# Moving the start addresses of on-chip tiles in a one-core transformer layer: three filler tiles

## What is computed

```python
m = silu(cond) @ w_mod + b_mod            # six rows of 2048 for each of two conditions
z = (x * (1 + sc1) + sh1) @ w_in          # 8 heads q, k, v; latent q 512, latent kv 512, rope key 64
o = concat(neighbourhood_attention(z), mla_attention(z)) @ w_o
x = layernorm(ALPHA * x + g1 * o)
gate, up = split((x * (1 + sc2) + sh2) @ w_gu)   # 2 x 5632 columns
y = layernorm(ALPHA * x + g2 * (silu(gate) * up) @ w_down)
```

## Time and profile before

| | |
|---|---|
| median of 3 runs | 2891.59 us (2889.24 to 2893.04) |
| span of the profiled execution | 2891.1 us |
| TensorE matmul busy | 2814.6 us, 97% |
| TensorE weight load busy | 2494.9 us, 86% |
| VectorE busy | 1889.6 us, 65% |
| ScalarE busy | 1043.8 us, 36% |
| GpSimd busy | 187.9 us, 6% |
| mean granted TensorE clock | 0.987 |

### The profile page before, as it was taken

One profiled execution on the slowest core, in us unless ns is written; L12 is line 12 of the kernel. 1 busy time (PEld: TensorE's weight loads), 2 busy tenths in 40 slices (PEclk: granted clock), 3 DMA queues, 4 the chain that ended last, 5 costly groups with the idle time before them and its releaser, 6 DMA issues.

```text
span 2891.1 us, 42097 instructions
## 1 busy us (share of the span) xinstructions
PE 2814.6 (97%) x15844; PEld 2494.9 (86%) x15844; DVE 1889.6 (65%) x2939; ACT 1043.8 (36%) x1814; POOL 187.9 (6%) x262
## 2 busy tenths in 40 slices
PE   7899999999999999799999999999999999999996
PEld 2679999877888776799999999999999888888885
DVE  8766666585885787866666666666666555424337
ACT  7422333224453213644444444444444312112121
POOL 1121111000001000000000000000000000000005
PEclk9999999999999999899999999999999999999998
DMA  9754333352334655122222222222222535223231
GB/s 383 274 186 154 125 128 132 122 191 71 104 110 173 220 175 182 63 101 97 101 101 101 99 98 101 101 99 92 96 101 101 198 119 174 80 89 137 80 124 73
DMA packets 105768, 379.82 MB, mean 131 GB/s; under 512 B 14062, under 2 KB 14466, under 8 KB 103754
## 3 DMA queue, kind: packets, MB, share of 16 engines
q1 hardware_dynamic: 89088, 317.36, 30.9%
q0 software_dynamic: 16000, 61.06, 6.0%
q10 hardware_dynamic: 586, 0.12, 0.0%
HBM read 346.97 MB, written 33.48 MB: 132 GB/s over the span
## 4 chain that ended last, share of the span: by engine, by line
PE 90%; DVE 4%; DMA 2%; ACT 2%; issue 1%; SPq 0%; ACTq 0%; DVEq 0%
PE ps L1955 16%; PE ps L1957 16%; PE ps L1956 16%; PE ps L2455 12%; PE ps L2453 12%; PE ps L2454 12%; DMA mraw<-in_wstream 2%; PE ps L2154 1%; PE ps L2119 1%; DVE ps L1883 1%; PE ps L2102 1%; DVE acc L1885 1%; DVE stat L1933 0%; PE ps L2150 0%; PE ps L2093 0%
## 5 line engine op out<-in xcount | busy, mean ns | idle before, releaser
L2453 PE MATMUL ps<-actl,ringh 128*128 128x320 f32 x1408 | 435.5, 309 | 3.9 <-DVE ringl L1754 3.9
L2454 PE MATMUL ps<-acth,ringh 128*128 128x320 f32 x1408 | 435.1, 309 | 0.0
L2455 PE MATMUL ps<-actl,ringl 128*128 128x320 f32 x1408 | 435.1, 309 | 0.0
L2453 PE MATMUL ps<-acth,ringh 128*128 128x320 f32 x1056 | 327.1, 310 | 7.6 <-DVE ringl L1754 7.6
L2454 PE MATMUL ps<-actl,ringh 128*128 128x320 f32 x1056 | 326.9, 310 | 0.0
L2455 PE MATMUL ps<-acth,ringl 128*128 128x320 f32 x1056 | 326.8, 309 | 0.0
L1955 PE MATMUL ps<-dwh,fring 128*128 128x512 f32 x820 | 319.4, 390 | 1.0 <-DVE dwl L1858 1.0
L1957 PE MATMUL ps<-dwh,fring 128*128 128x512 f32 x820 | 319.2, 389 | 0.0
L1956 PE MATMUL ps<-dwl,fring 128*128 128x512 f32 x820 | 319.1, 389 | 0.0
L1858 DVE TENSOR_TENSOR dwl<-raw,dwh 128x1024 fp32r<-128x1024 f32 x82 | 100.4, 1224 | 291.4 <-ACT dwh L1319 291.4
L1754 DVE TENSOR_TENSOR ringl<-raw,ringh 128x512 fp32r<-128x512 f32 x264 | 181.7, 689 | 162.8 <-ACT ringh L1253 162.8
(11 more groups left out here) (310 smaller groups left out, 5775.0 us busy)
## 6 DMA issues: line engine op xcount, KB each, us to landing
raw<-in_wstream SPq DMA_DIRECT2D x503, 512.0 KB, 3.3
mraw<-in_wstream SPq DMA_DIRECT2D x64, 512.0 KB, 7.7
fscr<-fst POOLq DMA_DIRECT2D x44, 320.0 KB, 2.4
fst<-fscr SPq DMA_DIRECT2D x21, 640.0 KB, 4.1
acc<-in_xT SPq DMA_DIRECT2D x8, 640.0 KB, 16.0
oscr<-ost POOLq DMA_DIRECT2D x16, 320.0 KB, 2.5
ostage<-oscr POOLq DMA_DIRECT2D x16, 320.0 KB, 3.9
acc<-in_xtok POOLq DMA_DIRECT2D x4, 1280.0 KB, 7.4
```

The costliest lines, as they stand in the source:

```text
L2453: mm(out, ringh[:, s, w], ah, start=first, stop=False, skip_group_check=True)
L2454: mm(out, ringh[:, s, w], al, start=False, stop=False, skip_group_check=True)
L2455: ins = mm(out, ringl[:, s, w], ah, start=False, stop=last, skip_group_check=True)
```

## The change

Three tiles that nothing reads or writes are added, so that later tiles start elsewhere. No instruction is added, removed or moved: on each of the five engines the built program lists the same operations on the same tiles in the same order.

```diff
@@ -211,6 +211,7 @@
         bcols2 = sb("bcols2", [P, 2 * KD], f32, wsc)
         conds = sb("conds", [P, 2, KD, 2], f32, wsc)
         unit = sb("unit", [P, 3], f32, wsc)
+        sb("to_128", [P, 24], f32, wsc)
         grow = sb("grow", [2, 512], f32, wsc)
         mod1 = sb("mod1", [P, 2 * KD, 2], f32, wsc)
 
@@ -289,9 +290,10 @@
 
         f2 = ExitStack()
         fring = sb("fring", [P, 7, 2, 2, T], f32r, f2)
+        sb("dw_to_2k", [P, 32], f32, f2)
         dwh = sb("dwh", [P, 2, 1024], f32r, f2)
         dwl = sb("dwl", [P, 2, 1024], f32r, f2)
-        pad0 = sb("pad0", [P, 20480 // 4 - 4096], f32, f2)
+        pad0 = sb("pad0", [P, 20480 // 4 - 4096 - 32], f32, f2)
         gate2 = sb("gate2", [P, 2, D], f32, f2)
         tmp2 = sb("tmp2", [P, 2, 512], f32, f2)
         rowsb = sb("rowsb", [P, D], f32, f2)
@@ -304,6 +306,7 @@
         xsc.close()
 
         ysc = ExitStack()
+        sb("ring_to_2k", [P, 32], f32, ysc)
         ringh = sb("ringh", [P, 4, 512], f32r, ysc)
         ringl = sb("ringl", [P, 4, 512], f32r, ysc)
         xb = sb("xb", [P, 8, P], f32, ysc)
```

## The result

The changed kernel takes 2897.74 us (median of 13 runs, 2894.4 to 2899.43), the kernel before 2892.92 us (median of 13 runs on the same chips, 2889.24 to 2893.57). The ratio is 1.0016 with a 95% interval of 1.0009 to 1.0024: some 5 us slower, within the 0.2% that the prediction counts as no change, and not the 14 us faster that it forecast. The profiled execution after took 2897.18 us with a span of 2895.6 us, so 1.6 us lie outside its span. That holds for the kernel before too: of its later runs, the one of 2892.57 us has a span of 2891.0. The text ahead of the prediction set its span of 2891.1 us beside the median without this difference, which puts the forecast about 1 us too low and changes nothing else.

A forecast was written before the change was run, and what follows sets the result against it. TensorE, busy 97% of the span, was taken as the bound, through how fast matmuls follow each other. 6.4 + 6.4 + 1.2 + 0.8 - 0.8 = 14.0 us off 2891.1 gave 2877.1, as median 2877.6 us; range 2872 to 2893.

The forecast's parts named there:

- The step that failed: 512-column fp32r matmuls: each pays some 7 ns when its stationary slice starts off a multiple of 128 bytes.
- the moving operand does not seem to matter: Moving operand's address has no effect: 320-column matmuls with it 32 bytes off run 146.7 ns, gate and up's pace.
- `hh`: Values and latent projections: 320 triples gain 20 ns each, 6.4 us, by taking the remainders of the fast down projection.
- `oh`: Output projection: 320 triples gain 6.4 us, as `oh` comes to remainder 256, a multiple of 128.
- `ckvh`, `qlh` and the scores: Stages reading `ckvh` and `qlh` gain 1.2 us, latent attention's score matmuls 0.8 us, from addresses at multiples of 128.
- The rings: Gate and up (`ringh`) and down projection (`dwh`): moving the rings to multiples of 2048 bytes changes nothing, 0 us.
- The moved `dwh` loses: Rival, down projection: the distance between both operands' remainders counts, so 16.4 us are lost, time 2894; chance 0.05.
- What is late next: Two chunk ends: TensorE's shorter blocks wait for VectorE's split, 0.4 us more each, giving back 0.8 us.
- a rule against any gain: The skill's 16-byte SBUF lines and address-independent matmul pace (216 ns at 512 columns): no stage gains, sum 0.

The follow-up runs named there:

- e8_widths: Not the layer: the streams of e4_table with 256 to 512 moving columns, and with plain fp32; one run, 745.5 us.
- e4_table: Not the layer: TensorE alone runs fp32r streams, 128 stationary and 512 moving columns, at 16 x 16 start remainders; one run, 1692.5 us.
- e5_off32: e3_oh384 with `whi`, `hh`, `oh`, `ckvh` and `qlh` together 32 bytes off a multiple of 128; 2880.32 us, ratio 0.9959 to the kernel before.
- e6_dw256: e3_oh384 with `dwh` and `dwl` 256 bytes further on, `fring` unmoved; 2879.19 us, ratio 0.9955 to the kernel before.
- e3_oh384: e1_to128 plus a filler of 128 bytes ahead of `oh`, so `oh` meets `whi` at difference 0; 2879.12 us, ratio 0.9956 to the kernel before.
- e2_rings: The kernel before with the two ring fillers alone, without `to_128`; 2907.12 us, ratio 1.0051.
- e7_scores: e3_oh384 with `mx` and `rs` placed earlier, moving `qh` and `kh` to remainder 384 by 512; 2880.98 us, ratio 0.9960 to the kernel before.
- e1_to128: The kernel before with the filler `to_128` alone, both rings where they were; 2883.52 us against 2892.57, ratio 0.9970.

## Why the prediction was wrong

**The step that failed** is the sentence in bold: that a matmul pays when its stationary slice starts off a multiple of 128 bytes, with "the moving operand does not seem to matter" behind it. It rested on one contrast, the down projection (384 against 384) with the others (288 or 160 against 384). In that contrast the stationary remainder and the difference between both operands change together, so it can't tell them apart. What seemed to exclude the moving operand was taken at 320 columns, where e8_widths shows the same pace at every difference: the comparison could not have come out otherwise. What counts, at 512 columns, is the difference by 256 bytes: some 227 ns at 0 against 232.4 at 128 and 233.3 at 96 and 224 (e4_table, e5_off32, e6_dw256).

**`hh`, right.** The term "copies a measured case", and so it held under either rule, which makes its success no evidence for the one in bold: 6.4 us forecast, 3.1 + 2.6 = 5.7 us measured. By the table it is 960 x (233.4 - 227.7) = 5.5 us.

**`oh`, mis-sized through the same step.** 6.4 us forecast, 2.3 us measured. The argument "before, `oh` at 160 and `hh` at 288 paid the same" had a second reading: both were at a bad difference, 224 and 96. The change took `oh` to 128, a third bad one. The table gives 960 x (233.3 - 232.4) = 0.9 us, and the steps of the stage itself at full clock fall by as much, from 233.3 to 232.4 ns on average. The rest, 1.4 us, is the shorter time at the lower clock (1.5 us, less 0.1 us of longer waits), which e2_rings has as well without any change to this stage's addresses: so even the 2.3 us are in good part luck. With difference 0 (e3_oh384) the stage is 6.9 us shorter than before, as the term had it.

**`ckvh`, `qlh` and the scores.** 1.2 us forecast, 1.1 us measured. Scores: 0.8 us forecast, 0.1 us measured. The filler moves both operands of each by the same 96 bytes, so their difference stayed what it was, 128 between `kl_` and `qh`. With that at 0 (e7_scores) the stage gives 0.4 us.

**The rings.** For `ringh` the 0 was right: 684 matmuls in 100 us, 1090.63 us for the stage. For `dwh` it was not, +13.8 us. The mechanism stood in the text as the rival *The moved `dwh` loses*, at 16.4 us, and got a chance of 0.05. The steps of the timelines, 232.2 after against 226.7 in the earlier trace rows, give 2460 x 5.5 = 13.5 us. That rival's time was 2894, with all the gains of the forecast left in. By its own rule `oh` and the scores gain nothing (6.4 and 0.8 us), and then nothing is given back at the chunk ends (0.8 us), which I had not worked through: 2894 + 6.4 + 0.8 - 0.8 gives 2900, beside 2898 measured. It was given too little: the 0 for `dwh` copied no case, since no large operand of the trace before stood at remainder 0, and the same text noted that.

**What is late next, right in kind, but not reached.** VectorE's split at two chunk ends was to cost TensorE 0.4 us each once its blocks were shorter. In the changed kernel they hardly were, and the two waits together came to 0.9 us, beside 0.41 + 0.39 = 0.8 us before. In e3_oh384, where the blocks are as short as forecast, they are 0.65 and 0.78 us, the second of which was 0.39 us in the earlier trace rows.

The Trainium skill was weighed in the prediction as a rule against any gain. By its page SBUF — State Buffer (Who interferes with whom), TensorE has two independent read ports, one for the moving operand and one for weight loads. From that alone one would expect no effect of where the two stand to each other. The trace shows one with all else idle, 226.7 against 233.4 ns (e4_table); whether it arises at the ports no run shows. The 16-byte lines of the same page (Specifications) give no reason for it either, since every address here is a multiple of 32. The 216 ns that the prediction took from TensorE: Matmul & The Clock Gate (Back-to-back issue gap) is that section's figure for an isolated matmul; the best stream here takes 226.7 ns.

**What stays open** is whether a matmul's own two operands are the pair that counts or its moving operand and the next one's stationary slice, since all three matmuls of a triple had the same remainders in every run that decides; which part of the memory or of TensorE's fetch has the period of 256 bytes, why difference 64 pays only 1.6 ns, and the 0.9 us that the changed kernel starts later (99.62 to 100.54 us at the first value matmul; the tiles in use up to there have the same addresses in e1_to128, which has 99.38 us).

## What to carry to other kernels

For a stream of fp32r matmuls with 128 stationary and 512 moving columns, list for each operand pair the difference between the two start addresses by 256 bytes and bring it to 0; 2.9% of the pace of such a stage hangs on it, and a round address of one operand alone brings nothing and can spoil a pair that was good. Stages of 320 moving columns, and plain fp32 at 512, showed no effect; with 64 or 32 stationary columns difference 0 brought nothing. A contrast between two stages shows that something differs, not what: before a rule is read from it, list everything that differs between them, test a suspect where the effect exists, and where it can be done measure the grid by itself: 256 pairs took one run of 1.7 ms here.

## What the runs showed of the hardware

All at a granted clock of 1.00 but for the 427 ns, which is a step at 0.50. Two streams of triples with 128 stationary and 512 moving columns that differ only in the addresses of their operands run at 226.7 or up to 234.2 ns a matmul. Even the best pair stays 13.3 ns above 512 / 2.4 = 213.3 ns. At 320 columns the excess is the same 13.3 ns whatever the addresses (146.7 against 133.3), and plain fp32 takes 429.2 ns at 512 columns at the four pairs tried.
